# VectorE's small steps of the differential attention as steps of their own, with four slots for the small tiles

## The chip, the cores and the metric

The kernel runs on one core of one Trainium2 chip. The metric is the device time of one execution in microseconds. The engines of the core are TensorE (PE in the rows, its weight loads PEld), VectorE (DVE), ScalarE (ACT), GpSimd (POOL) and SyncE (SP), which issues most of the transfers. Each has an instruction stream of its own; they meet only through semaphores.

## The reference, cut to what matters

The block holds projections, differential attention with 4 heads, latent attention with 4 heads, an output projection and an MLP. The change touches the differential attention alone. For one head, with 2064 keys (16 meta tokens and 2048 tokens):

```python
s1 = einsum(q1, k1) * scale + bias      # bias: ALiBi slope * distance, and the chunk mask
s2 = einsum(q2, k2) * scale + bias
a = softmax(s1) - lam * softmax(s2)
o = einsum(a, v)
```

`lam` is one number for all heads, made of two dot products and two exponentials.

## The kernel before

The queries of a head are 16 tiles of 128 rows, i = 0 to 15, in four groups g of four tiles. Tile i sees 16 + 128*(i+1) keys (144 for tile 0, 2064 for tile 15). Each tile has two components c (`s1` and `s2`), and each component's scores are cut into chunks of at most 512 columns: one chunk for tiles 0 to 2, two for 3 to 6, three for 7 to 10, four for 11 to 14, five for 15. That makes 88 chunks a head, numbered 0 to 87: tile 3 begins at chunk 6, tile 7 at 22, tile 8 at 28, tile 11 at 46, tile 12 at 54, tile 13 at 62, tile 14 at 70, tile 15 at 78.

What the engines do for one tile:

- TensorE makes a chunk's scores in one of four PSUM banks (line 1609, two passes of fp32r). Before chunk n it waits until VectorE has read chunk n - 4.
- VectorE reads a chunk out of its bank (line 1531): it adds the bias, writes the row into SBUF and keeps the chunk's maximum. After a component's last chunk it makes the negative maximum of the row (line 1538).
- ScalarE takes the exponential of the row in place and sums it (line 1477). This needs the maximum.
- "scale": VectorE makes the inverse of the first sum (`invert`, line 1563); GpSimd multiplies the first row by it (line 1469).
- "end": VectorE makes the inverse of the second sum (line 1570), multiplies it by minus lambda (line 1572), and adds the second row, times that, to the first (line 1576, one pass over the whole row).
- "turn": TensorE transposes the finished rows of a group, one key tile at a time (line 1642), into one of three banks; ScalarE copies it out (line 1490). The first turn of group g waits for the end of its last tile, 4g + 3.
- "product": TensorE multiplies the transposed tile with the values (line 1656), and ScalarE copies the group's sum out ("out", line 1497).

Group 3 of a head has its turns and products beside the first rows of the next head. All engines follow one list of steps, made by `row_steps` (the order of chunks, exponentials, scales and ends) and `head_steps` (which spreads turns and products over it by a cost of each step). Each engine walks the list and does its own kinds of step. A step of a row is put off by a number of chunks: the exponential 1, the scale `SCALE_AFTER` = 2, the end `END_AFTER` = 5; at the last chunk of a component of tile i, whatever is still due for tiles below i is put there at once. The first turn of a group is held back in the list until the end that it needs has passed.

Rows of the first component lie in `rows`; those of the second in `second`, which has two slots, tile i in slot i % 2. The small tiles `mx`, `nmax`, `total`, `inv` and `inv2` have two slots as well.

Of the kernel before, what the change touches and what calls it, by code (L numbers as in the profile page):

```python
# [30 lines left out]
P = 128  # L31
D = 1024
SEQ = 2048
META = 16
# [1128 lines left out]
def attention(nc, io, scr, ident, ahead, latent):  # L1163
# [8 lines left out]
    with ExitStack() as ctx:  # L1172
# [10 lines left out]
        mx = mem.sb("da_mx", [P, 2, COMPS, 5])  # L1183
        nmax = mem.sb("da_nmax", [P, 2, COMPS])
        nmax_all = mem.sb("da_nmax_all", [P, 5])
        total = mem.sb("da_total", [P, 2, COMPS])
        inv = mem.sb("da_inv", [P, 2, COMPS])
        inv2 = mem.sb("da_inv2", [P, 2])
# [15 lines left out]
        inv2_step = mem.sem("da_inv2_step")  # L1204
# [58 lines left out]
        def cost(step):  # L1263
# [3 lines left out]
            return META + P * (step[2] + 1) + 250 if step[0] == "end" else 0  # L1267
# [47 lines left out]
        SCALE_AFTER, END_AFTER = 2, 5  # L1315
# [146 lines left out]
        def _(pool):  # L1462
# [3 lines left out]
            def scaled(h, i, u, **at):  # L1466

                hold(pool, inv_ready, NT * h + i + 1)
                pool.tensor_scalar(row(i, u), row(i, u), inv[:, i % 2, 0:1], 1.0, ALU.mult, ALU.mult).then_inc(first_scaled, 1)
# [4 lines left out]
        def _(act):  # L1474
            def exp(h, i, c, u, **at):
                act.wait_ge(max_ready, NT * COMPS * h + COMPS * i + c + 1)
                act.activation(comp_row(i, c, u), comp_row(i, c, u), ACT.Exp, bias=nmax[:, i % 2, c:c + 1], scale=scale,
                               accum_out=total[:, i % 2, c:c + 1]).then_inc(exp_ready, 1)
# [32 lines left out]
        def _(dve):  # L1511
            def chunk(h, n, pair, u):
# [7 lines left out]
                if i % 4 == 0 and c == 0 and k0 == 0:  # L1520
# [4 lines left out]
                    elif g != 1 and not first_head:  # L1525
# [3 lines left out]

                hold(dve, scores_ready, NCH * h + n + 1)  # L1530
# [3 lines left out]
                                         accum_out=mx[:, i % 2, c, nth:nth + 1]).then_inc(scores_read, 1)  # L1534
                if k0 + w == META + P * (i + 1):
                    dve.wait_ge(scores_read, NCH * h + n + 1)

# [1936 lines left out]
```

## Time and profile before

| | us |
|---|---|
| median of 3 runs | 2602.93 |
| lowest, highest | 2600.15, 2602.96 |
| profiled execution, from its first to its last instruction | 2600.7 |
| differential attention in it | 432 to 799 |
| latent attention, output projection, MLP | from 802 on |

The page gives the profiled execution's own time as its span, and nothing that lies around it. In the whole span TensorE is busy for 98%, VectorE 62%, ScalarE 47%, GpSimd 13%. Times of rows are microseconds from the span's start. In the timeline rows the columns are start, duration, engine, line, operation, result and operands with the shape, how many were merged into the row, and in brackets the idle time before it with the engine that ended it. TensorE's passes are pipelined: a transposition seen alone takes 0.27 us, four in a row 0.60 us.

### The profile page before, as it was taken

How to read it: one execution, taken by the hardware profiler on the slowest of the kernel's cores; microseconds unless marked ns; L12 is line 12 of the kernel's file. 1: busy time of each engine (PE TensorE's matmuls, PEld its weight loads, DVE VectorE, ACT ScalarE, POOL GpSimd, SP SyncE). 2: the span in 40 equal slices, each digit the busy share in tenths (PEclk: the TensorE clock that was granted, in tenths of full speed). 3: DMA queues.
4: the chain of work that ended last, by engine and by line, in shares of the span. 5: the costliest groups of instructions: out<-in, count | busy, mean ns of one | idle time of the engine just before them, and what ended most of it. 6: DMA issues, size and time to landing. Idle time of an engine off the chain costs nothing.

```text
span 2600.7 us, 35372 instructions
## 1 busy us (share of the span) xinstructions
PE 2540.5 (98%) x12220; PEld 2114.9 (81%) x12220; DVE 1614.7 (62%) x3499; ACT 1212.5 (47%) x2183; POOL 332.0 (13%) x368
## 2 busy tenths in 40 slices
PE   8999999999999999999999999999999999999997
PEld 7998888777667999977877888888888888888886
DVE  6123306998995776654458677876757465564765
ACT  6112314777764555554544333533335353443554
POOL 1110002222221222210000000000000001111143
PEclk9999999999999999999999999999999999999999
DMA  7334458553332111135677767657655365776787
GB/s 232 122 106 125 126 163 253 143 135 87 93 131 90 36 31 45 41 110 158 194 247 220 221 200 237 218 182 216 190 161 179 110 221 108 171 167 162 203 162 137
DMA packets 329436, 398.59 MB, mean 153 GB/s; under 512 B 21408, under 2 KB 235664, under 8 KB 320944
## 3 DMA queue, kind: packets, MB, share of 16 engines
q1 hardware_dynamic: 311696, 364.41, 44.7%
q0 software_dynamic: 17568, 31.99, 8.4%
q8 instruction: 95, 1.56, 0.2%
q14 instruction: 77, 0.63, 0.1%
HBM read 239.86 MB, written 156.48 MB: 152 GB/s over the span
## 4 chain that ended last, share of the span: by engine, by line
PE 62%; DVE 3%; DMA 1%; ACT 1%; issue 1%; SPq 0%; POOL 0%; DVEq 0%; ACTq 0%; POOLq 0%
PE ff_ps_x L3262 26%; PE ff_ps_m L3262 13%; PE ff_ps_z L3262 6%; PE ml_ps_s L2139 6%; PE ff_ps_m L1695 4%; PE ml_ps_o L2168 4%; PE ml_ps_t L2152 2%; DMA ml_v_raw<-scr_yT 1%; DMA ff_pieces<-scr_acc 0%; PE ff_ps_r L2699 0%; PE mo_ps_t L2716 0%; SPq L2326 0%; DVE ff_pieces L2429 0%; DVE ff_pieces L2620 0%; DVE ff_pieces L2616 0%
## 5 line engine op out<-in xcount | busy, mean ns | idle before, releaser
L3262 PE MATMUL ff_ps_x<-ff_mv_hi_p,ff_st_hi_p 128*128 128x512 f32 x764 | 297.8, 390 | 0.5 <-ACT ff_u L3002 0.5
L3262 PE MATMUL ff_ps_x<-ff_mv_hi_p,ff_st_lo_p 128*128 128x512 f32 x764 | 297.3, 389 | 0.0
L3262 PE MATMUL ff_ps_x<-ff_mv_lo_p,ff_st_hi_p 128*128 128x512 f32 x764 | 297.2, 389 | 0.0
L2139 PE MATMUL ml_ps_s<-wide,ml_qs 128*128 128x416 f32 (+14 forms) x880 | 195.6, 356 | 3.7 <-PEq L137 2.7
L3108 DVE TENSOR_TENSOR ff_st_lo_p<-ff_ps_m,ff_st_hi_p 128x512 fp32r<-128x512 f32 x190 | 130.8, 689 | 103.4 <-ACT ff_st_hi_p L2985 103.4
L2952 POOL DMA_DIRECT2D scr_acc<-ff_pieces x64 | 55.5, 872 | 1015.3 <-DVE ff_pieces L3132 946.9
L3002 ACT ACTIVATE ff_u<-ff_ps_x 128x512 f32<-128x512 f32 x128 | 76.6, 598 | 215.0 <-PE ff_ps_x L3262 215.0
L3262 PEld LDWEIGHTS ff_ps_x<-ff_mv_hi_p,ff_st_hi_p 128*128 128x128 f32 x764 | 143.4, 188 | 32.4 <-issue 2.0
L3262 PEld LDWEIGHTS ff_ps_x<-ff_mv_hi_p,ff_st_lo_p 128*128 128x128 f32 x764 | 143.4, 188 | 29.9
L3262 PEld LDWEIGHTS ff_ps_x<-ff_mv_lo_p,ff_st_hi_p 128*128 128x128 f32 x764 | 143.4, 188 | 29.6
L2139 PEld LDWEIGHTS ml_ps_s<-wide,ml_qs 128*128 128x128 f32 x880 | 152.0, 191 | 16.3 <-issue 2.9
L2985 ACT ACTIVATE ff_st_hi_p<-st_raw 128x512 fp32r<-128x512 f32 x191 | 119.4, 626 | 86.3 <-PE ff_ps_z L3262 86.3
L3262 PE MATMUL ff_ps_m<-wide,ff_st_hi_p 128*128 128x512 f32 x512 | 157.7, 389 | 0.4 <-DVE ff_st_lo_p L2603 0.4
L2985 ACT ACTIVATE ff_st_hi_p<-ff_ps_m 128x512 fp32r<-128x512 f32 x190 | 113.2, 598 | 93.7 <-PE ff_ps_m L3262 93.7
L3262 PE MATMUL ff_ps_x<-wide,ff_st_hi_p 128*128 128x512 f32 x504 | 155.1, 389 | 0.0
L3108 DVE TENSOR_TENSOR ff_st_lo_p<-st_raw,ff_st_hi_p 128x512 fp32r<-128x512 f32 x191 | 131.0, 688 | 36.9 <-ACT ff_st_hi_p L2985 35.6
L2054 DVE CUSTOM_DVE_ANT_0 ml_rows<-ml_ps_s,ahead_bias 128x416 f32<-128x416 f32 (+14 forms) x176 | 100.2, 570 | 72.1 <-PE ml_ps_s L2139 64.2
L1656 PE MATMUL da_ps_o<-da_pT,da_v 128*128 128x512 f32 (+3 forms) x320 | 137.2, 529 | 0.0
L1977 ACT ACTIVATE ml_pT_hi<-ml_ps_t 128x512 fp32r<-128x512 f32 (+3 forms) x176 | 90.7, 538 | 93.4 <-PE ml_ps_t L2152 93.0
L2076 DVE TENSOR_TENSOR ml_pT_lo<-ml_ps_t,ml_pT_hi 128x512 fp32r<-128x512 f32 (+3 forms) x176 | 105.3, 616 | 41.6 <-ACT ml_pT_hi L1977 41.2
L1609 PE MATMUL da_ps_s<-da_keys,ahead_q 128*128 128x416 f32 (+14 forms) x352 | 112.6, 423 | 2.4 <-DVE da_mx L1531 2.4
L3262 PEld LDWEIGHTS ff_ps_m<-wide,ff_st_hi_p 128*128 128x128 f32 x512 | 96.0, 188 | 20.5 <-issue 0.6
(318 smaller groups left out, 6349.7 us busy)
## 6 DMA issues: line engine op xcount, KB each, us to landing
st_raw<-in_w_ff SPq DMA_DIRECT2D x64, 512.0 KB, 6.2
scr_hid<-ff_pieces SPq DMA_DIRECT2D x128, 256.0 KB, 2.7
st_raw<-scr_hid SPq DMA_DIRECT2D x64, 512.0 KB, 5.4
ring<-in_w_ff SPq DMA_DIRECT2D x28, 1024.0 KB, 7.7
scr_t<-ring SPq DMA_DIRECT2D x24, 1024.0 KB, 5.8
ring<-scr_t SPq DMA_DIRECT2D x21, 1024.0 KB, 8.1
scr_acc<-ff_pieces POOLq DMA_DIRECT2D x64, 256.0 KB, 4.1
ring<-scr_u SPq DMA_DIRECT2D x13, 1024.0 KB, 8.4
```

What stands on the lines that cost most here:

```text
L1609: m = pe.matmul(ps_s[n % NSB][:, 0:w], qs[:, g % 2, c, P * b:P * b + P], keys[u][:, 2 * c + j, k0:k0 + w], start=j == 0, stop=j == 1)
L1656: pe.matmul(ps_o[:, c0:512], v_meta[:, :] if t == 0 else v[:, t - 1], pT[0:rows_of, n % NPT, c0:512], start=t == 0, stop=t == tiles_of(g) ...
L1695: m = pe.matmul(bank, y[a][:, k], w[b][:, cols], start=k == 0 and i == 0, stop=k == KD - 1 and i == 2, skip_group_check=True)
L1977: act.activation(pT_hi[0:rows_of, n % NPT, c0:512], ps_t[n % NTB][0:rows_of, c0:512], ACT.Copy).then_inc(hi_copied, 1)
L2054: dve.tensor_tensor_reduce(out=row(i, u)[:, k0:k0 + w], in0=ps_s[n % NSB][:, 0:w], in1=bias[:, b0:b0 + w], scale=1.0, scalar=LOWEST, op0=A ...
L2076: dve.tensor_tensor(pT_lo[0:rows_of, n % NPT, c0:512], ps_t[n % NTB][0:rows_of, c0:512], f32(pT_hi[0:rows_of, n % NPT, c0:512]), ALU.subtr ...
L2139: m = pe.matmul(ps_s[n % NSB][:, 0:w], q, k, start=j == 0, stop=j == len(pairs) - 1)
L2168: m = pe.matmul(ps_o[:, c0:512], v[0:rows_of, at_v], p, start=t == 0 and j == 0, stop=t == tiles_of(g) - 1 and j == 2)
L2985: act.activation(st_hi[kind][:, :, :], stationary(kind, n % 2), ACT.Copy).then_inc(st_hi_ready, 1)
L3002: act.activation(tile, bank[:, :], ACT.Copy).then_inc(taken, 1)
L3108: dve.tensor_tensor(st_lo[kind][:, :, :], stationary(kind, n % 2), f32(st_hi[kind][:, :, :]), ALU.subtract).then_inc(st_lo_ready, 1)
L3262: m = pe.matmul(bank[:, :], w[kind][:, k], a[kind][:, k], start=start and k == 0 and i == 0, stop=stop and k == KH - 1 and i == 2, skip_gr ...
```

## The change

It has three parts.

1. The negative maximum of a row becomes a step of its own, "most". It was made right behind the last chunk of a component; now one chunk later, right ahead of its exponential. Its long output goes back into `mx`, and `nmax_all` is dropped.
2. The end is cut in three: "invert" (the second inverse), "weigh" (the product with minus lambda) and "end" (the addition), each put off by one chunk more than the one before. The invert is put off by 5 chunks for tile 15, 3 for tiles 0 to 2, else by two less than the number of chunks of the next tile's two components, at most 6; so the addition comes 2 chunks after that. `SCALE_AFTER` becomes 3. What is still due at a component's last chunk is put there only from one tile further back than before in the first component, and not at all for tiles 0 to 2.
3. The small tiles get four slots (i % 4), and the rows of the second component of tiles 0 to 2 lie side by side in slot 0. Since in-order work no longer guards the second rows, VectorE waits for `probs_ready` ahead of the first chunk of each second component.

In the planner the cost of an end falls from its width + 250 to its width + 100.

```diff
-        mx = mem.sb("da_mx", [P, 2, COMPS, 5])
+        mx = mem.sb("da_mx", [P, 4, COMPS, 5])
...
         def comp_row(i, c, u):
-            return row(i, u) if c == 0 else second[:, i % 2, 0:META + P * (i + 1)]
+            if c == 0:
+                return row(i, u)
+            start, wide = (sum(META + P * (a + 1) for a in range(i)), 0) if i < 3 else (0, i % 2)
+            return second[:, wide, start:start + META + P * (i + 1)]
...
-                        steps += [step for _, step in later if step[2] - NT * step[1] < i]
-                        later = [(left, step) for left, step in later if step[2] - NT * step[1] >= i]
-                        later.append((1, ("exp", 0, i, c)))
+                        due = i if c == COMPS - 1 else i - 1
+                        if i < 3:
+                            due = -1
+                        steps += [step for _, step in later if step[2] - NT * step[1] < due]
+                        later = [(left, step) for left, step in later if step[2] - NT * step[1] >= due]
+                        later += [(1, ("most", 0, i, c)), (1, ("exp", 0, i, c))]
                         if c == 0:
                             later.append((SCALE_AFTER, ("scale", 0, i)))
                         if c == COMPS - 1:
-                            later.append((END_AFTER, ("end", 0, i)))
+                            later += [(after, (kind, 0, i)) for kind, after in zip(("invert", "weigh", "end"), end_after(i))]
...
+        def end_after(i):
+            first = {NT - 1: 5, 0: 3, 1: 3, 2: 3}.get(i) or min(6, 2 * len(row_chunks(i + 1)) - 2)
+            return first, first + 1, first + 2
...
-        SCALE_AFTER, END_AFTER = 2, 5
+        SCALE_AFTER = 3
...
+                if c == 1 and k0 == 0 and not (first_head and i < 4):
+                    dve.wait_ge(probs_ready, NT * h + (-1 if i < 3 else 0 if i == 3 else i - 1))
...
+            def most(h, i, c, **at):
+                last = max(n for n, chunk in enumerate(chunks) if chunk[:2] == (i, c))
+                parts = len(row_chunks(i))
+                dve.wait_ge(scores_read, NCH * h + last + 1)
+                dve.tensor_scalar(mx[:, i % 4, c, 0:parts], mx[:, i % 4, c, 0:parts], -scale, None, ALU.mult, ALU.min,
+                                  accum_out=nmax[:, i % 4, c:c + 1]).then_inc(max_ready, 1)
...
+            def invert_second(h, i, **at):
+                dve.wait_ge(exp_ready, NT * COMPS * h + COMPS * (i + 1))
+                dve.reciprocal(inv[:, i % 4, 1:2], total[:, i % 4, 1:2]).then_inc(second_inverted, 1)
+
+            def weigh_second(h, i, **at):
+                dve.wait_ge(second_inverted, NT * h + i + 1)
+                dve.tensor_scalar(inv2[:, i % 4:i % 4 + 1], inv[:, i % 4, 1:2], lam[:, 3:4], None, ALU.mult).then_inc(second_weighed, 1)
+
+            def end(h, i, u, **at):
+                dve.wait_ge(second_weighed, NT * h + i + 1)
+                dve.wait_ge(first_scaled, NT * h + i + 1)
+                dve.scalar_tensor_tensor(out=row(i, u), in0=comp_row(i, 1, u), scalar=inv2[:, i % 4:i % 4 + 1], in1=row(i, u),
+                                         op0=ALU.mult, op1=ALU.add).then_inc(probs_ready, 1)
```

## Rows read from the trace of the kernel before

**Rows 1.** The page's first part: busy time and share of the span.

```profile
PE 2540.5 (98%) x12220; PEld 2114.9 (81%) x12220; DVE 1614.7 (62%) x3499; ACT 1212.5 (47%) x2183; POOL 332.0 (13%) x368
```

**Rows 2.** Window within the differential attention: stretch, busy time by engine, clock, DMA.

```profile
602.00:685.00 83.00, 80.06 (x407) 59.48 (x406) 76.78 (x293) 60.73 (x108) 17.72 (x16) 1.00 0.45 108
```

**Rows 3.** Waits from 432 to 775: who, for whom, us, times, longest.

```profile
ACT da_second L1477 <- DVE da_nmax_all L1538: 44.0, 39, 2.9
DVE da_inv L1570 <- ACT da_second L1477: 6.7, 4, 2.2
PE da_ps_s L1609 <- DVE da_mx L1531: 6.1, 10, 1.1
```

**Rows 4.** Timeline of PE: what its passes take, and two waits further in.

```profile
458.36 1.92 PE L1609 MATMUL da_ps_s<-wide,ahead_q 128*128 128x336 f32 x10
460.12 0.60 PE L1642 MATMUL da_ps_t<-ident,da_rows 128*128 128x128 f32 x4
...
463.63 0.67 PE L1609 MATMUL da_ps_s<-wide,ahead_q 128*128 128x448 f32 x2 [1.07 <-DVE da_mx L1531]
...
561.22 0.64 PE L1609 MATMUL da_ps_s<-da_keys,ahead_q 128*128 128x416 f32 x2 [0.45 <-DVE da_mx L1531]
...
586.24 1.02 PE L1656 MATMUL da_ps_o<-da_pT,da_v 128*128 128x512 f32 x2
```

**Rows 5.** Timeline of PE where head 1 ends and head 2 starts.

```profile
597.15 0.63 PE L1609 MATMUL da_ps_s<-da_keys,ahead_q 128*128 128x400 f32 x2 [0.75 <-DVE da_mx L1531]
...
604.43 1.09 PE L1642 MATMUL da_ps_t<-ident,da_rows 128*128 128x128 f32 x8 [1.26 <-DVE da_rows L1576]
...
607.07 1.12 PE L1656 MATMUL da_ps_o<-da_pT,da_v_meta 128*128 128x512 f32 x2 [0.48 <-ACT da_pT L1490]
```

**Rows 6.** Timeline of DVE over the same change of heads.

```profile
597.52 0.09 DVE L1531 DVE_READ_ACCUMULATOR2_ANT da_mx<- 128x1 f32 x1
597.52 0.16 DVE L1563 RECIPROCAL da_inv<-da_total 128x1 f32<-128x1 f32 x1
597.60 0.57 DVE L1531 CUSTOM_DVE_ANT_0 da_second<-da_ps_s,da_bias 128x416 f32<-128x416 f32 x1
...
598.09 0.59 DVE L1531 CUSTOM_DVE_ANT_0 da_second<-da_ps_s,da_bias 128x416 f32<-128x416 f32 x1
...
599.10 0.09 DVE L1531 DVE_READ_ACCUMULATOR2_ANT da_mx<- 128x1 f32 x1
599.22 0.16 DVE L1538 TENSOR_SCALAR_CACHE_REDUCE da_nmax_all<-da_mx 128x5 f32<-128x5 f32 x1
599.30 0.08 DVE L1538 DVE_READ_ACCUMULATOR da_nmax_all<-da_mx 128x1 f32 x1
...
601.56 0.16 DVE L1570 RECIPROCAL da_inv<-da_total 128x1 f32<-128x1 f32 x1 [1.61 <-ACT da_second L1477]
601.76 0.21 DVE L1572 TENSOR_SCALAR da_inv<-da_inv,da_lam 128x1 f32<-128x1 f32 x1
602.01 2.37 DVE L1576 SCALAR_TENSOR_TENSOR da_rows<-da_second,da_inv,da_rows 128x2064 f32<-128x2064 f32 x1
604.29 0.30 DVE L1531 CUSTOM_DVE_ANT_0 da_second<-da_ps_s,ahead_bias 128x144 f32<-128x144 f32 x1
```

**Rows 7.** Timeline of DVE: chunk 57 of head 1, which had to wait for its scores.

```profile
571.13 0.51 DVE L1531 CUSTOM_DVE_ANT_0 da_rows<-da_ps_s,da_bias 128x336 f32<-128x336 f32 x1 [0.42 <-PE da_ps_s L1609]
```

**Rows 8.** Timeline of ACT over the same change of heads.

```profile
599.42 2.02 ACT L1477 ACTIVATE da_second<-da_second,da_nmax 128x2064 f32<-128x2064 f32 x1 [2.65 <-DVE da_nmax_all L1538]
601.34 0.19 ACT L1477 ACTIVATION_READ_ACCUMULATOR da_second<-da_second,da_nmax 128x1 f32 x1
601.44 0.40 ACT L1477 ACTIVATE da_rows<-da_rows,da_nmax 128x144 f32<-128x144 f32 x1
```

**Rows 9.** Windows at the end of the stage, where PE stands idle and starts again.

```profile
775.00:778.00 3.00, 0.68 (x6) 0.68 (x7) 2.97 (x3) 0.18 (x1) 0.00 (x0) 1.00 0.25 94
778.00:782.00 4.00, 4.00 (x15) 2.72 (x14) 3.60 (x7) 1.86 (x4) 0.00 (x0) 0.57 0.32 68
```

More of the change, by code:

```diff
@@ L1182, in attention @@
         pT = mem.sb(f"da_pT", [P, NPT, 512])
-        mx = mem.sb("da_mx", [P, 2, COMPS, 5])
[L1184 to L1188, printed above, removed]
+        mx = mem.sb("da_mx", [P, 4, COMPS, 5])
+        nmax = mem.sb("da_nmax", [P, 4, COMPS])
+        total = mem.sb("da_total", [P, 4, COMPS])
+        inv = mem.sb("da_inv", [P, 4, COMPS])
+        inv2 = mem.sb("da_inv2", [P, 4])
         lam = mem.sb("da_lam", [P, 4])
@@ L1203, in attention @@
         inv_ready, first_scaled, probs_ready = (mem.sem(f"da_{s}") for s in ("inv_ready", "first_scaled", "probs_ready"))
-        inv2_step = mem.sem("da_inv2_step")
+        second_inverted, second_weighed = mem.sem("da_second_inverted"), mem.sem("da_second_weighed")
         pT_ready, pv_done = mem.sem(f"da_pT_ready"), mem.sem("da_pv_done")
@@ L1266, in cost @@
                 return chunks[step[2]][3] + 60
-            return META + P * (step[2] + 1) + 250 if step[0] == "end" else 0
+            return META + P * (step[2] + 1) + 100 if step[0] == "end" else 0
         def head_steps():
@@ L1468, in scaled @@
                 hold(pool, inv_ready, NT * h + i + 1)
-                pool.tensor_scalar(row(i, u), row(i, u), inv[:, i % 2, 0:1], 1.0, ALU.mult, ALU.mult).then_inc(first_scaled, 1)
+                pool.tensor_scalar(row(i, u), row(i, u), inv[:, i % 4, 0:1], 1.0, ALU.mult, ALU.mult).then_inc(first_scaled, 1)
             heads(pool, {"scale": scaled})
@@ L1476, in exp @@
                 act.wait_ge(max_ready, NT * COMPS * h + COMPS * i + c + 1)
-                act.activation(comp_row(i, c, u), comp_row(i, c, u), ACT.Exp, bias=nmax[:, i % 2, c:c + 1], scale=scale,
-                               accum_out=total[:, i % 2, c:c + 1]).then_inc(exp_ready, 1)
+                act.activation(comp_row(i, c, u), comp_row(i, c, u), ACT.Exp, bias=nmax[:, i % 4, c:c + 1], scale=scale,
+                               accum_out=total[:, i % 4, c:c + 1]).then_inc(exp_ready, 1)
                 if isinstance(h, int) and (h, i, c) == (0, 0, 1):
@@ L1555, in minus_lambda, with invert_first @@
                 dve.wait_ge(lam_step, 4)
-            def invert(h, i, u, **at):
+            def invert_first(h, i, u, **at):
                 dve.wait_ge(exp_ready, NT * COMPS * h + COMPS * i + 1)
-                if not (isinstance(h, int) and h == 0 and i < 2):
-                    dve.wait_ge(first_scaled, NT * h + i - 1)
-                dve.reciprocal(inv[:, i % 2, 0:1], total[:, i % 2, 0:1]).then_inc(inv_ready, 1)
-            def end(h, i, u, **at):
+                if not (isinstance(h, int) and h == 0 and i < 4):
+                    dve.wait_ge(first_scaled, NT * h + i - 3)
+                dve.reciprocal(inv[:, i % 4, 0:1], total[:, i % 4, 0:1]).then_inc(inv_ready, 1)
@@ L1574, in end @@
                 dve.wait_ge(first_scaled, NT * h + i + 1)
-                dve.scalar_tensor_tensor(out=row(i, u), in0=comp_row(i, 1, u), scalar=inv2[:, i % 2:i % 2 + 1], in1=row(i, u),
+                dve.scalar_tensor_tensor(out=row(i, u), in0=comp_row(i, 1, u), scalar=inv2[:, i % 4:i % 4 + 1], in1=row(i, u),
                                          op0=ALU.mult, op1=ALU.add).then_inc(probs_ready, 1)
-            heads(dve, {"chunk": chunk, "scale": invert, "end": end})
+            heads(dve, {"chunk": chunk, "most": most, "scale": invert_first, "invert": invert_second, "weigh": weigh_second, "end": end})
```

12 lines of the change are left out of this document (1 added, 11 removed).

## The prediction

> **What bounds the kernel now.** I read the page's busy shares first, then windows over the stage of the change, then the waits, then the timelines of the engines where one head meets the next. Over the whole span TensorE is the busy one [rows 1]. In the stage of the change it is busy for 80.06 of 83 us and VectorE for 76.78 [rows 2]: two engines, both near their limit, so each needs its own sum. The waits go both ways: TensorE for VectorE's reads 6.1 us, VectorE for ScalarE's exponential 6.7, ScalarE for VectorE's maxima 44.0 [rows 3].
>
> TensorE's work of a head. Ten score passes take 1.92 us, of which the last 0.30 is a tail, so a pass costs 0.18 us; four transpositions take 0.60 us and one alone 0.27, so one costs 0.11; a product is two passes, 0.43 apart (1.02 less the 0.59 of one), so 0.86 at full width [rows 4]. A head has 176 score passes (31.7 us), 152 transpositions (16.7 us), and products worth 38 full ones (32.7 us): 81 us. The four heads take 343 us from 432 to 775, 85.8 each. TensorE thus stands still for some 4.7 us a head.
>
> Where it does, in a head further in: ahead of chunk 87 (0.75 us, waiting for VectorE), ahead of the first turn of group 3 (1.26, waiting for the end of tile 15), ahead of that group's first product (0.48, for ScalarE's copy) [rows 5], and ahead of chunk 47 (0.45) [rows 4]. Each costs some 0.25 more than it prints, because after a gap the overlap of passes is lost: 1.0, 1.5, 0.75 and 0.7. With small ones of 0.6 in all (chunks 0, 70 and 79) that makes 4.6. Head 0 has no old group to turn, and loses 1.3 ahead of chunk 35 (1.07 printed) [rows 4], 0.7 ahead of chunk 47, and 1.0 in its first ten chunks. After the last head it waits 3.0 for the last end. Sum up to 777 us: 3.0 in head 0, 0.4 in each of the four third groups, 3.5 at each of three changes of head, 2.2 at chunk 47 of three heads, 4.0 at the close: 21.3 us. Nothing that the change does to VectorE can give back more.
>
> VectorE's work of a head. A read costs its columns at 0.96 per ns plus 0.08, about 0.5 us for 416 (chunk at 597.60, next at 598.09). A maximum costs 0.24: the read's accumulator goes out at 599.10, the maximum starts at 599.22, its own accumulator at 599.30, the next work 0.04 later. An end costs 0.45 before its long pass (601.56 to 602.01), then its columns plus 0.1 [rows 6]. A head: 43.8 for reads, 32 maxima 7.7, 16 inverses 1.2, 16 ends 27.2, together 80 us.
>
> **What the change does to VectorE.** The 0.12 between 599.10 and 599.22 is the wait for its own result: an inverse that has nothing to wait for starts in the same instant as the accumulator before it, and costs 0.08 (597.52 to 597.60) [rows 6]. One chunk later, the maximum has nothing to wait for either: 0.085 in place of 0.24, 5.0 us over 32. The inverse and the lambda product of an end fall from 0.45 to 0.08 plus the product's cost by itself, which no row shows; it lies between 0.08 (as an inverse) and 0.25 (its start to the addition's, with the wait), and I take 0.13, nearer to an operation without a wait: 3.9 us over 16. VectorE's head goes from 80 to 71 us, 36 us less over the stage (31 to 37 by the two ends). The added wait ahead of each second component costs nothing: the end that it asks for lies three or more chunks back in the list. The copy of the maximum into `mx` and the four slots move no work. ScalarE gets each maximum one read (0.5 us) later, and the copies queued behind its exponentials with it; its 44.0 us of waiting for maxima [rows 3] cover that, since a product asks for a copy two or more turns back. SyncE's loads and GpSimd's scaling wait for counts that come no sooner and, by 1 us at most, later; GpSimd is idle most of the time.
>
> The page "VectorE: DVE Perf Modes" of the Trainium skill, section "The DRAIN you can't avoid", speaks against this saving: a next operation starts only when the pipe is empty, and a semaphore in between "costs nothing extra". The row shows 0.12 us where there is a wait and nothing where there is none, so I go by the row; by the page the sum of VectorE would stay at 80 us.
>
> **What it does to TensorE.** VectorE was not alone in setting the pace, so its 36 us aren't the gain. At chunk 57 it already waits 0.42 for scores [rows 7]; with less work it sits directly behind TensorE over most of a head, and TensorE stops only where an order of steps makes it. I walked the new list with the costs above, in four places.
>
> Chunk 47 and head 0. The end of tile 9 comes after chunk 45 in place of 42, and VectorE is 3 us ahead of where it was. The 0.7 at chunk 47 goes in all heads, and about 1.1 of the 2.3 that head 0 loses in its first ten chunks and at chunk 35: 3.9 us gained.
>
> Chunk 61. The end of tile 11 is put off from chunk 57 to chunk 61, and the first turn of group 2, which was at 60, is held back to stand right behind it. VectorE starts to read chunk 61 0.15 us after its scores at best and some 0.6 with the lag that I get; the read costs 0.43, the addition 1.72. TensorE has 0.65 us of products left and then stands until that end: 2.7 less 0.65, 2.1 us (1.6 at best). It did not wait here before. Four heads: 8.4 us lost. ScalarE has the copies of group 1 behind it and adds nothing.
>
> Chunks 70 to 85. The scale of tiles 11 to 14 is two chunks behind the maximum, 1.2 to 1.4 us of work, and asks for an exponential of up to 2.0 us: VectorE now stands here for some 0.6 us at tiles 13 and 14, where an end used to cover it. TensorE, up to four banks ahead, loses 0.3 a head, as much as it did before (0.4). Even.
>
> The change of heads. With the end of TensorE's chunk 85 as zero: VectorE has read it at 1.8, makes the end of tile 14 (2.1), which was at chunk 82 before, and reads 86, 87 and chunk 0 of the next head until 5.2. The maximum of tile 15 follows at 5.3; before it was at 4.2, ahead of chunk 0. The exponential with its accumulator, from there to the inverse, takes 2.3 (599.22 to 601.56), and that of tile 0 another 0.4 [rows 6, 8]. VectorE's scale of tile 0, which the list has ahead of all that is left of tile 15, waits for it until 7.9: the 1.61 of idle time returns in another place. Then it has chunks 4, 5 and 6 and nine small steps, 2.2 us, and only then the end of tile 15, 2.25 with its tail: 12.5. TensorE has by then chunks 86 to 6 of the next head and eight products, three of them narrow, 8.2 us. It stands still for 4.3 us, in two pieces (0.7 ahead of chunk 2, which needs the bank of chunk 86, the rest ahead of the first turn). Three turns then stand before the first product, so the 0.75 for the copy goes. 4.3 against 3.5: three times 0.8 lost, 2.4 us. At the close of the last head VectorE reads chunk 87 1.1 later and TensorE has 1.0 more work to hide it: even.
>
> Sum: -3.9 + 8.4 + 0 + 2.4 - 0.4 (the small ones) = +6.5 us. What follows, from 777 on, only moves: no transfer of those stages ends a wait of TensorE's in this one. The page gives the profiled execution as 2600.7 us and nothing around it; the median is 2602.9, so I set 2609.
>
> **Rivals.** Faster: VectorE's reads decide after all. If VectorE's 9 us a head let it stand right behind TensorE at chunk 61 and at the change of heads too, its lateness costs nothing: the waits ahead of chunks 35, 47 and 87 go (1.3 + 2.8 + 4.0), the small ones too (1.6), and the two new ones shrink to what the end itself takes; 2594. For it: both waits for `da_mx` ahead of chunks 47 and 87 are of this kind. Against: an end of 2 us still stands in one piece before the first turns. It decides if the new wait at chunk 61 is under 0.5 us. Chance 0.25.
>
> No change: the lag behind TensorE is 0.15 in place of what I carried (-0.4 a head at chunk 61, -1 at the change of heads), some 5 us less: 2603. Chance 0.29.
>
> Slower still, by the clock: TensorE's idle time of 2.8 us at 775 is followed by a stretch at 0.57 of its clock, half speed in most of 4 us [rows 9], a loss of some 1.7 us; the 1.5 us of idle time at 604 is not. I get 3.6 in one piece at three changes of head: +5, 2614. Chance 0.12, as the piece may be shorter.
>
> That waits cost VectorE nothing, as the page has it: the ends are later by the same chunks, and the path from chunk 57 to the end of tile 15 grows by what I had taken off it, ten maxima by 0.155 and five ends by 0.25, 2.8 us: +11, 2620. The 0.12 of the row would then be something else. Chance 0.04.
>
> **Numbers.** My forecast (chance 0.30): 2609, in a range of its own of 2605 to 2612. A measurement of this kernel tells some 0.2%, 5.2 us, from no change: faster is below 2597.7, slower above 2608.1. The two cases above the forecast lie in slower, with three quarters of the forecast's; the rest of it, the no-change case and a fifth of the faster one lie within: faster 0.21, same 0.41, slower 0.38. The range runs from 2593, the faster rival, to 2616, past the clock's.
>
> **What would show it.** Right: reads right after `TENSOR_SCALAR_CACHE_REDUCE` with no 0.12 before it, VectorE's busy time in the stage some 20 us lower; a wait of PE for `da_rows` in every head between the product of width 128 after chunk 61 and the first turn, some 2 us; one of over 2.5 at the change of heads; no wait ahead of chunk 47. Wrong: no wait at chunk 61, or waits for `da_mx` that add up to more than now.

## The result, and the profile after

The changed kernel takes 2637.78 us (median of four runs, 2635.87 to 2639.6), the kernel before 2601.54 in the same comparison: a ratio of 1.0142 [1.013, 1.0154]. It is 36 us slower. The forecast of 2609 had the direction and a fifth of the size, and the time lies 22 us outside its range.

All of it is lost in the stage of the change. From the first scores of the differential attention to the first of the latent attention the trace of before takes 369.9 us (432.2 to 802.1), that of after 405.1 (431.8 to 836.9). The 1798 us behind it are alike. The windows of the stage in the trace of before (length; busy us and instructions of PE, PEld, DVE, ACT, POOL; granted clock; DMA share; GB/s):

```profile
432.00:802.00 370.00, 353.14 (x1738) 260.47 (x1736) 318.94 (x1232) 260.72 (x463) 77.42 (x67) 1.00 0.47 124
```

The page's busy line of the kernel after, which answers to [rows 1], hides it: the shares are within a point of the old ones.

```profile
PE 2551.9 (97%) x12220; PEld 2124.8 (81%) x12220; DVE 1621.2 (62%) x3499; ACT 1213.2 (46%) x2183; POOL 335.6 (13%) x368
```

The windows of the same trace show it, first the stretch that answers to [rows 2], then the whole stage:

```profile
602.00:685.00 83.00, 73.54 (x359) 54.37 (x358) 69.38 (x270) 54.41 (x101) 17.45 (x15) 0.97 0.47 115
...
432.00:837.00 405.00, 360.87 (x1736) 267.18 (x1736) 325.68 (x1231) 260.22 (x462) 78.00 (x67) 0.97 0.42 113
```

TensorE is busy for 73.5 of 83 us where it was busy for 80.1 [rows 2]. VectorE's busy time in the stage was to fall by some 20 us. It rose, from 318.94 to 325.68. That one number says that something has become slower, for the change takes no pass away from GpSimd and adds none to VectorE.

The waits from 432 to 810 (engine and line waiting, releaser: us, times, longest) have the one of TensorE for the finished rows, which was not among those of any size in [rows 3]. ScalarE's for the maxima is up from 44.0 us:

```profile
ACT da_second L1487 <- DVE da_mx L1556: 59.5, 36, 3.6
...
PE da_ps_t L1661 <- DVE da_rows L1595: 22.1, 7, 3.9
PE da_ps_s L1628 <- DVE da_mx L1544: 14.3, 12, 1.8
```

VectorE's timeline from the inverse of tile 11 on (start, us, engine, line, operation, result and operands; idle time and its releaser in brackets) shows both halves of the story:

```profile
575.00 0.16 DVE L1579 RECIPROCAL da_inv<-da_total 128x1 f32<-128x1 f32 x1 [0.43 <-ACT da_rows L1487]
575.12 0.47 DVE L1544 CUSTOM_DVE_ANT_0 da_second<-da_ps_s,da_bias 128x304 f32<-128x304 f32 x1
575.52 0.08 DVE L1544 DVE_READ_ACCUMULATOR2_ANT da_mx<- 128x1 f32 x1
575.52 2.87 DVE L1595 SCALAR_TENSOR_TENSOR da_rows<-da_second,da_inv,da_rows 128x1424 f32<-128x1424 f32 x1
578.32 0.61 DVE L1544 CUSTOM_DVE_ANT_0 da_rows<-da_ps_s,da_bias 128x448 f32<-128x448 f32 x1
578.86 0.07 DVE L1544 DVE_READ_ACCUMULATOR2_ANT da_mx<- 128x1 f32 x1
578.86 0.14 DVE L1556 TENSOR_SCALAR_CACHE_REDUCE da_mx<-da_mx 128x4 f32<-128x4 f32 x1
...
583.03 0.21 DVE L1589 TENSOR_SCALAR da_inv<-da_inv,da_lam 128x1 f32<-128x1 f32 x1
583.15 0.15 DVE L1579 RECIPROCAL da_inv<-da_total 128x1 f32<-128x1 f32 x1
```

The small steps do what they were said to: the maximum starts in the same instant as the accumulator before it (578.86), with no 0.12 between them, and the lambda product costs 0.12 (583.03 to 583.15; 0.13 was assumed). But the addition over 1424 columns (tile 10) takes 2.87 us, where the same form took 1.70 before. The prediction's rule, columns at 0.96 per ns and 0.1, gives 1.58 up to the start of the next operation, which comes some 0.1 us ahead of the printed end. GpSimd in the same stretch:

```profile
575.33 1.58 POOL L1479 TENSOR_SCALAR da_rows<-da_rows,da_inv 128x1552 f32<-128x1552 f32 x1 [3.35 <-DVE da_inv L1579]
```

GpSimd's scaling of tile 11 (1552 columns) begins 0.2 us ahead of VectorE's addition for tile 10 and ends at 576.91; the addition is longer than its 1.70 by 1.17, out of 1.39 us beside each other. The additions of tiles 13 to 10, once in each of the four heads, in the groups by form (count, busy us, mean ns, idle before), ahead of the change:

```profile
L1576 DVE SCALAR_TENSOR_TENSOR da_rows<-da_second,da_inv,da_rows 128x1808 f32<-128x1808 f32 x4 | 8.4, 2101 | 0.1
L1576 DVE SCALAR_TENSOR_TENSOR da_rows<-da_second,da_inv,da_rows 128x1680 f32<-128x1680 f32 x4 | 7.9, 1970 | 0.1
L1576 DVE SCALAR_TENSOR_TENSOR da_rows<-da_second,da_inv,da_rows 128x1552 f32<-128x1552 f32 x4 | 7.3, 1835 | 0.1
L1576 DVE SCALAR_TENSOR_TENSOR da_rows<-da_second,da_inv,da_rows 128x1424 f32<-128x1424 f32 x4 | 6.8, 1703 | 0.1
```

and after it:

```profile
L1595 DVE SCALAR_TENSOR_TENSOR da_rows<-da_second,da_inv,da_rows 128x1808 f32<-128x1808 f32 x4 | 13.9, 3482 | 0.0
L1595 DVE SCALAR_TENSOR_TENSOR da_rows<-da_second,da_inv,da_rows 128x1680 f32<-128x1680 f32 x4 | 13.1, 3266 | 0.0
L1595 DVE SCALAR_TENSOR_TENSOR da_rows<-da_second,da_inv,da_rows 128x1552 f32<-128x1552 f32 x4 | 12.3, 3081 | 0.0
L1595 DVE SCALAR_TENSOR_TENSOR da_rows<-da_second,da_inv,da_rows 128x1424 f32<-128x1424 f32 x4 | 11.5, 2870 | 0.0
```

From 7.61 us a head to 12.70: 5.1 more, 20.4 over four heads. Of the others only that of tile 15 is longer by more than 0.02 us, 2.44 for 2.37. Why these four: the scale stood two chunks behind its maximum and now stands three behind, the ends moved as well, and the two have met: for i = 11 to 14 the list now has the scale of tile i right ahead of the addition of tile i - 1.

Where that comes out is TensorE's timeline. From the first turn of group 2 in head 1 to the first of group 3:

```profile
582.13 0.81 PE L1675 MATMUL da_ps_o<-da_pT,da_v 128*128 128x256 f32 x4
...
586.82 0.66 PE L1661 MATMUL da_ps_t<-ident,da_rows 128*128 128x128 f32 x4 [3.87 <-DVE da_rows L1595]
...
608.57 1.75 PE L1628 MATMUL da_ps_s<-da_keys,ahead_q 128*128 128x400 f32 x6 [1.83 <-DVE da_mx L1544]
...
615.19 0.52 PE L1628 MATMUL da_ps_s<-wide,ahead_q 128*128 128x272 f32 x2 [1.30 <-DVE da_mx L1544]
...
623.16 1.53 PE L1661 MATMUL da_ps_t<-ident,da_rows 128*128 128x128 f32 x12 [2.34 <-DVE da_rows L1595]
```

After the narrow products these are idle pieces of one head: ahead of the first turn of group 2, ahead of chunk 82, and two at the change of heads. Counted from the ends of passes, as in the prediction, a head further in loses 4.1 us ahead of the first turn of group 2, 0.8 and 2.1 in chunks 70 to 85, 0.5 at chunk 49, 1.6 ahead of chunk 2 and 2.6 ahead of the first turn of group 3: 11.7 in place of 4.6, some 28 us over four heads. The rest of the 35 is the clock. The window behind the first of these waits:

```profile
586.00:592.00 6.00, 5.18 (x23) 4.63 (x24) 3.13 (x10) 3.47 (x5) 0.00 (x0) 0.72 0.43 103
```

Inside it, from 588.1 to 591.5, the granted clock is 0.50. Such stretches, of 3.4 us if nothing else is said, begin at 492.5, 588.1, 680.2 (6.8 us long), 779.2 and 813.4, 20 us in all, each behind a wait of TensorE's (the one at 680.2 begins 1.8 us before its wait ends); the kernel before has one in the stage, of 3.4 us at 778.1 [rows 9]. Half speed over 17 us more is at most 8.5 us of work lost, and 28 + 8.5 is the 35 to within 2. The two windows of the whole stage divide it alike: TensorE's idle time rises from 16.9 to 44.1 us, its busy time from 353.1 to 360.9.

### The profile page after: what moved, and what is told of

Same layout as the page of the kernel before. It is cut to its first block, busy times and chain, and to the rows that moved or that the text cites. A ratio compares the mean times of both kernels' runs of the same rounds, so it can differ in the third digit from the quotient of the medians.

```text
span 2634.1 us, 35370 instructions
## 1 busy us (share of the span) xinstructions
PE 2551.9 (97%) x12220; PEld 2124.8 (81%) x12220; DVE 1621.2 (62%) x3499; ACT 1213.2 (46%) x2183; POOL 335.6 (13%) x368
## 3 DMA queue, kind: packets, MB, share of 16 engines
q8 instruction: 95, 1.56, 0.2%
## 4 chain that ended last, share of the span: by engine, by line
PE 61%; DVE 2%; DMA 1%; ACT 1%; issue 1%; SPq 0%; POOL 0%; DVEq 0%; ACTq 0%; POOLq 0%
PE ff_ps_x L3281 25%; PE ff_ps_m L3281 13%; PE ff_ps_z L3281 6%; PE ml_ps_s L2158 6%; PE ff_ps_m L1714 4%; PE ml_ps_o L2187 4%; PE ml_ps_t L2171 2%; DMA ml_v_raw<-scr_yT 1%; DMA ff_pieces<-scr_acc 0%; PE ff_ps_r L2718 0%; PE mo_ps_t L2735 0%; SPq L2345 0%; DVE ff_pieces L2448 0%; DVE ff_pieces L2639 0%; DVE ff_pieces L2635 0%
## 5 line engine op out<-in xcount | busy, mean ns | idle before, releaser
L1628 PE MATMUL da_ps_s<-da_keys,ahead_q 128*128 128x416 f32 (+14 forms) x352 | 120.1, 441 | 7.4 <-DVE da_mx L1544 7.4
L1661 PE MATMUL da_ps_t<-ident,da_rows 128*128 128x128 f32 x608 | 95.5, 281 | 25.6 <-DVE da_rows L1595 25.6
```

The source lines that it names most:

```text
L1628: m = pe.matmul(ps_s[n % NSB][:, 0:w], qs[:, g % 2, c, P * b:P * b + P], keys[u][:, 2 * c + j, k0:k0 + w], start=j == 0, stop=j == 1)
L1661: m = pe.transpose(ps_t[n % NTB][0:rows_of, P * b:P * b + P], row(4 * g + b, u)[:, k0:k0 + rows_of], ident[:, :])
```

## The experiments

Theory C (collision): a pass of GpSimd that has started makes the addition beside it wait. Theory O (order): the ends' new places alone cost TensorE the time. All edits are to the changed kernel; where one stands on top of another, the text says so. A difference between two experiments is one of their medians, unless the profiled executions are named.

**The scale behind the addition.** The scale of tiles 11 to 14 is put off by one chunk more, which puts it behind the addition of the tile before.

```diff
-                            later.append((SCALE_AFTER, ("scale", 0, i)))
+                            later.append((4 if 11 <= i <= 14 else SCALE_AFTER, ("scale", 0, i)))
```

> The changed kernel, with the scale of tiles 11 to 14 put off by one chunk more, so that it stands right behind the addition of the tile before instead of right ahead of it. Theory (two engines at one port): in the changed kernel GpSimd's pass over a row starts 0.2 us before VectorE's addition, and the addition of tiles 10 to 13 takes 2.87 to 3.48 us instead of 1.70 to 2.10; apart again they take 1.7 to 2.1, which gives back at least the 20.4 us that were added, and with TensorE's half-clock stretches some 25: 2610 to 2617. Rival (the order of steps alone costs the time, the long additions are hidden behind TensorE): all waits and all ends stay where they are, so 2630 or more.

Measured: 2616.85 us, ratio 1.0058 [1.0043, 1.0074]: 21 us come back. The longest of the four additions, by form:

```profile
L1595 DVE SCALAR_TENSOR_TENSOR da_rows<-da_second,da_inv,da_rows 128x1808 f32<-128x1808 f32 x4 | 8.4, 2099 | 0.0
```

And the timelines of VectorE and then of GpSimd, where tile 10's addition and tile 11's scale now follow one another:

```profile
570.14 1.70 DVE L1595 SCALAR_TENSOR_TENSOR da_rows<-da_second,da_inv,da_rows 128x1424 f32<-128x1424 f32 x1
...
572.43 0.62 DVE L1544 CUSTOM_DVE_ANT_0 da_rows<-da_ps_s,da_bias 128x448 f32<-128x448 f32 x1
```

```profile
572.07 1.56 POOL L1479 TENSOR_SCALAR da_rows<-da_rows,da_inv 128x1552 f32<-128x1552 f32 x1 [5.34 <-DVE da_inv L1579]
```

The read at 572.43 lies wholly beside GpSimd's pass and takes 0.62, as such reads do elsewhere (0.61 at 578.32 above). It has one operand in PSUM and one in SBUF; the addition has two in SBUF. Only the latter waits.

This is what the Trainium skill says on its page "SBUF — State Buffer", section "SBUF: two separate sides": VectorE with two SBUF inputs and GpSimd share a pair of ports, whichever starts first has it for its whole instruction, and "the other fully blocks". The trace of after agrees in place and, roughly, in size: the addition is 1.17 us longer for 1.39 us beside each other, 0.2 less than a block to the pass's end would give.

**GpSimd's pass made short.** The order of after is kept, and GpSimd scales only 16 columns; the rest of the scaling is left out.

```diff
-                pool.tensor_scalar(row(i, u), row(i, u), inv[:, i % 4, 0:1], 1.0, ALU.mult, ALU.mult)
+                pool.tensor_scalar(row(i, u)[:, 0:16], row(i, u)[:, 0:16], inv[:, i % 4, 0:1], 1.0, ALU.mult, ALU.mult)
```

> The changed kernel in its own order, with GpSimd's scaling done on 16 columns of each row instead of all of them (this part of the computation is left out). Theory (port): every addition takes what it takes alone, 1.70 us for 1424 columns and 2.10 for 1808, and the time falls by over 20 us, to 2608 to 2616. Rival (the additions are slow for what stands on VectorE itself, a wait or the new place of the rows): they stay at 2.9 to 3.5 us and the time within 3 us of 2638.

Measured: 2617.63, ratio 1.0062 [1.0047, 1.0078]. The additions by form:

```profile
L1595 DVE SCALAR_TENSOR_TENSOR da_rows<-da_second,da_inv,da_rows 128x1808 f32<-128x1808 f32 x4 | 8.4, 2097 | 0.0
...
L1595 DVE SCALAR_TENSOR_TENSOR da_rows<-da_second,da_inv,da_rows 128x1424 f32<-128x1424 f32 x4 | 6.8, 1697 | 0.0
```

With the order untouched the additions are back at their old length and the time is that of the experiment before. For these 20 us it is GpSimd's duration beside the additions that costs, not where the ends stand. Theory C holds for 21 of the 36 us.

**The old order with the new steps.** Splits and four slots stay; the places of scale and end are the old ones.

```diff
-                        due = i if c == COMPS - 1 else i - 1
-                        if i < 3:
-                            due = -1
+                        due = i
-            first = {NT - 1: 5, 0: 3, 1: 3, 2: 3}.get(i) or min(6, 2 * len(row_chunks(i + 1)) - 2)
+            first = 3
-            return META + P * (step[2] + 1) + 100 if step[0] == "end" else 0
+            return META + P * (step[2] + 1) + 250 if step[0] == "end" else 0
-        SCALE_AFTER = 3
+        SCALE_AFTER = 2
```

> The steps and the slots of the change, in the order of before: the maximum one chunk later, invert, weigh and end 3, 4 and 5 chunks behind, scale at 2, dues and costs as before. Theory: the splits save VectorE 9 us a head, and with the ends where they were TensorE loses none of the new waits, so the waits for VectorE's reads go: 2592 to 2597, ratio 0.996 to 0.998. Rival (a wait costs VectorE nothing): ratio 1.000, and the maximum still starts 0.1 us late. Second rival (the maximum one chunk later makes ScalarE late): slower, by up to 5 us.

Measured: 2675.24, ratio 1.029 [1.0276, 1.0304], the slowest of all. The theory and the first rival were wrong; the second rival had the direction, with 5 us at most where it became 75. The waits of the stage:

```profile
DVE da_inv L1577 <- ACT da_rows L1485: 56.9, 64, 1.7
...
DVE da_inv L1581 <- ACT da_second L1485: 44.8, 64, 2.2
```

VectorE now stands at each of the 64 first inverses and each of the 64 second ones for its exponential. The maximum comes a chunk later, so the exponential does; the scale that stayed two chunks behind the row has one chunk to wait out in place of two. `SCALE_AFTER = 3` belongs to the split; I had taken order and split to be separable. TensorE stands still for 58.6 of the stage's 443.3 us and is busy for 384.7 where it was for 353.1: with the waits came 51 us at half speed. The test of this reading is further down.

**Scale and tile 11's end.** The first experiment, with the end of tile 11 taken back to chunk 58.

```diff
-            first = {NT - 1: 5, 0: 3, 1: 3, 2: 3}.get(i) or min(6, 2 * len(row_chunks(i + 1)) - 2)
+            first = {NT - 1: 5, 0: 3, 1: 3, 2: 3, 11: 3}.get(i) or min(6, 2 * len(row_chunks(i + 1)) - 2)
```

> The first experiment of this set and, besides, the end of tile 11 put off by 5 chunks in all (chunk 58) instead of 8 (chunk 61). Theory: TensorE's wait ahead of the first turn of group 2 (4.1 us in the changed kernel, some 2.5 in the first experiment) goes in all four heads, 6 to 9 us less than the first experiment: 2602 to 2609. Rival (TensorE makes up for that wait later, because VectorE is the bound): within 2 us of the first experiment.

Measured: 2602.04 (ten runs, 2599.45 to 2606.69), ratio 1.0007 [0.9998, 1.0016]. The first turn of group 2, as the first experiment has it and as this one has it:

```profile
579.99 1.05 PE L1661 MATMUL da_ps_t<-ident,da_rows 128*128 128x128 f32 x4 [2.52 <-DVE da_rows L1595]
```

```profile
575.93 0.66 PE L1661 MATMUL da_ps_t<-ident,da_rows 128*128 128x128 f32 x4 [0.20 <-DVE da_rows L1595]
```

The wait of 2.5 us is down to 0.2. In the four heads the first experiment prints 2.17, 2.52, 2.17 and 2.17, so about 8.2 us go with them. The half-speed stretches of the stage are 17 us in the one trace and 13.6 in the other, up to 1.7 us more, and the profiled executions are 9.1 apart (2614.0 and 2604.9). The medians are 14.8 apart, and the rest goes with the clock: of the ten executions of this kernel the four with a mean granted clock of 0.994 took 2605.5 to 2606.7 us, the profiled one among them, and the six with 0.996 or 0.997 took 2599.5 to 2602.4. The four of the first experiment have 0.990, 0.992, 0.994 and 0.996 and took 2619.6, 2618.0, 2615.7 and 2609.6. Why the clock falls in one execution and not in the next is not shown.

**Tile 15's end sooner as well**, behind chunk 4 of the next head in place of 6.

```diff
-            first = {NT - 1: 5, 0: 3, 1: 3, 2: 3, 11: 3}.get(i) or min(6, 2 * len(row_chunks(i + 1)) - 2)
+            first = {NT - 1: 3, 0: 3, 1: 3, 2: 3, 11: 3}.get(i) or min(6, 2 * len(row_chunks(i + 1)) - 2)
```

> The kernel of the last experiment (scale of tiles 11 to 14 behind the sum, tile 11's end at chunk 58) with the end of tile 15 put off by 5 chunks instead of 7: behind chunk 4 of the next head, where it was behind chunk 6. Theory (TensorE waits 2.6 us at each change of heads only for where this end stands): the end comes 1.5 us sooner, three times, and TensorE's wait ahead of the first turn falls to about 1.0 us: 4 to 6 us less than before this edit, 2596 to 2599 where that kernel took 2602. Rival (VectorE has to wait for the exponential of tile 15 wherever the end stands): within 2 us of 2602.

Measured: 2598.06 (eleven runs), ratio 0.999 [0.9981, 0.9999], the lowest of all kernels, 0.1% below the one before. It is 4.0 us below the kernel that it stands on, as the theory had it, though the two intervals just touch. TensorE's timeline at its change of heads:

```profile
596.30 0.52 PE L1628 MATMUL da_ps_s<-wide,ahead_q 128*128 128x272 f32 x2 [1.20 <-DVE da_mx L1544]
...
602.91 0.66 PE L1661 MATMUL da_ps_t<-ident,da_rows 128*128 128x128 f32 x4 [1.60 <-DVE da_rows L1595]
```

Its stage by windows:

```profile
432.00:799.00 367.00, 349.17 (x1734) 261.11 (x1732) 302.44 (x1231) 258.66 (x462) 77.46 (x67) 0.99 0.47 125
```

VectorE is busy for 302.4 us in the stage, 16.5 fewer than before (318.94), and the stage is 2.6 us shorter (431.2 to 798.5).

**Tile 14's end sooner too**, behind chunk 83 in place of 85 (`14: 4` in the same table).

```diff
-            first = {NT - 1: 3, 0: 3, 1: 3, 2: 3, 11: 3}.get(i) or min(6, 2 * len(row_chunks(i + 1)) - 2)
+            first = {NT - 1: 3, 0: 3, 1: 3, 2: 3, 11: 3, 14: 4}.get(i) or min(6, 2 * len(row_chunks(i + 1)) - 2)
```

> The same and, besides, the end of tile 14 two chunks sooner, behind chunk 83 instead of 85. Theory: VectorE's 2.1 us addition then no longer stands between the reads of chunks 85 and 86, and TensorE's 1.5 us of waiting ahead of chunk 2 of the next head goes, 3 to 4 us less than with tile 15 alone: 2592 to 2596, faster than both kernels. Rival (the addition only moves, and TensorE then waits ahead of chunk 87 as in the kernel before, 1.0 us): 1 to 2 us less.

Measured: 2610.85, ratio 1.0041 [1.0027, 1.0055]: a loss of 12 us where a gain was expected. VectorE's timeline:

```profile
685.02 2.23 DVE L1595 SCALAR_TENSOR_TENSOR da_rows<-da_second,da_inv,da_rows 128x1936 f32<-128x1936 f32 x1
687.16 0.15 DVE L1556 TENSOR_SCALAR_CACHE_REDUCE da_mx<-da_mx 128x5 f32<-128x5 f32 x1
...
689.50 0.16 DVE L1579 RECIPROCAL da_inv<-da_total 128x1 f32<-128x1 f32 x1 [1.15 <-ACT da_rows L1487]
```

The end fell right ahead of the maximum of tile 15's first component, held it up by 2.2 us, and with it the exponential and the inverse that waits 1.15 us for it. TensorE's idle time in the stage is 4.5 us longer than without this edit (22.3 and 17.8), its busy time 7.0 (355.7 and 348.7): behind two waits close together, of 1.3 and 1.4 us, the granted clock is 0.50 for 3.4 us at all three changes of head (from 512.6, 601.4 and 690.1), which the kernel without this edit does not have.

**The maximum at once**, to weigh that split alone (to the kernel with scale and tile 11's end mended): `most` is called right behind the last read, as before the change.

```diff
+                if k0 + w == META + P * (i + 1):
+                    most(h, i, c)
-            heads(dve, {"chunk": chunk, "most": most, "scale": invert_first, "invert": invert_second, "weigh": weigh_second, "end": end})
+            heads(dve, {"chunk": chunk, "scale": invert_first, "invert": invert_second, "weigh": weigh_second, "end": end})
```

> The kernel of the last experiment of the first set (2602), with the maximum made right behind a component's last chunk again, in the same order of all other steps. It costs VectorE 0.155 us more each, 5 us a head, and gives ScalarE the maximum one read sooner. Theory (the split of the maximum brings nothing here, since TensorE is the bound and the exponential is what VectorE waits for): 2599 to 2603. Rival (VectorE's time counts): 2607 or more.

Measured: 2604.35, ratio 1.002 [1.0011, 1.003], 1.4 us above the range of the theory. The split of the maximum is worth 2.3 us by the medians; the intervals (that of its base reaches 1.0016) overlap, so it is not shown to be worth anything.

**The end in one piece**, on the same base: inverse and product stand right ahead of the addition again, with their waits.

```diff
+                invert_second(h, i)
+                weigh_second(h, i)
-            heads(dve, {"chunk": chunk, "most": most, "scale": invert_first, "invert": invert_second, "weigh": weigh_second, "end": end})
+            heads(dve, {"chunk": chunk, "most": most, "scale": invert_first, "end": end})
```

> The same kernel (2602), with invert and weigh right ahead of the addition again, each waiting for the one before, 0.25 us more for each of 16 ends of a head, the rest in the same order. Theory (only what stands ahead of a first turn or of a bank counts): 1 to 3 us more, 2603 to 2605. Rival (VectorE's time counts in full, 4 us a head): 2610 or more. Second rival (the sooner invert makes VectorE wait for exponentials and is itself the loss): 2600 or less.

Measured: 2609.15, ratio 1.0035 [1.0021, 1.0049]. This split is worth 7 us, more than the theory had and just under the rival's 2610. The intervals, up to 1.0016 and from 1.0021, are apart.

**Tile 14's end behind the maximum** (`14: 5`, behind chunk 84), to tell order from place in the loss above, and **tile 15's end behind chunk 3** (`NT - 1: 2`) on top of it.

```diff
-            first = {NT - 1: 3, 0: 3, 1: 3, 2: 3, 11: 3}.get(i) or min(6, 2 * len(row_chunks(i + 1)) - 2)
+            first = {NT - 1: 3, 0: 3, 1: 3, 2: 3, 11: 3, 14: 5}.get(i) or min(6, 2 * len(row_chunks(i + 1)) - 2)
```

> The kernel with tile 15's end behind chunk 4 (2598), with the end of tile 14 behind chunk 84 instead of 85. In the run that put it behind 83 it stood ahead of tile 15's maximum and made ScalarE's exponential, and with it the scale of tile 15, late (1.15 us of VectorE's idle time). Theory (that order was the loss, not the sooner end): here the maximum goes first, no wait for the exponential stands ahead of chunk 86, and TensorE's 1.5 us ahead of chunk 2 falls to about 1.0: 2594 to 2598. Rival (any sooner end of tile 14 costs): 2601 or more.

> The same with the end of tile 15 behind chunk 3. Theory: it stands ahead of the scale of tile 0 and its addition starts 0.6 us sooner; TensorE's wait ahead of the first turn falls from 1.8 to about 1.2 us: 1 to 3 us less than with chunk 4. Rival (its inverse at chunk 1 makes VectorE wait for the exponential before it has read chunks 2 and 3, and TensorE runs out of banks): 1 to 4 us more.

Measured: 2600.08, ratio 0.9997 [0.9988, 1.0006], and 2598.74, ratio 0.9995 [0.9986, 1.0004]. One chunk later, behind the maximum, the 11 us are back: it was the order, which set off the longer waits and the half-speed stretches behind them. The first lies between its theory (up to 2598) and its rival (from 2601) and decides nothing on the sooner end; the second is 1.3 us below it, as its theory had it. Neither can be told from the best kernel, nor from the kernel before: no place of the ends that was tried from here on gains anything that can be measured.

**The old order, with the maximum at once.** The third experiment with the edit of the seventh, `most` right behind the last read: if the late maximum made it slow, this cures it.

> The run that had the new steps in the order of before (2675), with the maximum made right behind the last chunk again; invert and weigh stay steps of their own. Theory (its loss was the maximum one chunk later with the scale still at 2: 64 waits for the first exponential of 0.9 us each and 64 for the second of 0.7): the waits for the first exponential fall to a few, those for the second by half, 2598 to 2608. Rival (the loss came from inverses that stand ahead of the reads): 2640 or more.

Measured: 2604.69, ratio 1.0012 [1.0003, 1.0022]; 70.6 us come back by one edit, as the theory had it. The waits:

```profile
DVE da_inv L1583 <- ACT da_second L1485: 10.4, 12, 2.2
...
DVE da_inv L1579 <- ACT da_rows L1485: 2.5, 3, 0.8
```

The 56.9 and 44.8 us are 2.5 and 10.4.

**The collision put back into the best kernel**, to size it where nothing else waits.

```diff
-                            later.append((4 if 11 <= i <= 14 else SCALE_AFTER, ("scale", 0, i)))
+                            later.append((SCALE_AFTER, ("scale", 0, i)))
```

> The kernel with tile 15's end behind chunk 4 (2598), with the scale of tiles 11 to 14 put back by one chunk, right ahead of the addition, as in the change. Theory (port): GpSimd's pass then meets three additions a head (tiles 10, 12 and 13; tile 11's stands elsewhere), 1.2 to 1.4 us each, 15.4 us in all, and most of it is on the path: 2608 to 2616, with tile 11's addition at 1.83 us. Rival (in an order without the two long waits TensorE covers it): within 3 us of 2598.

Measured: 2619.05, ratio 1.007 [1.0056, 1.0084], 21 us slower than without and 3 above the range of the theory. Its additions by form:

```profile
L1595 DVE SCALAR_TENSOR_TENSOR da_rows<-da_second,da_inv,da_rows 128x1808 f32<-128x1808 f32 x4 | 13.9, 3481 | 0.0
L1595 DVE SCALAR_TENSOR_TENSOR da_rows<-da_second,da_inv,da_rows 128x1680 f32<-128x1680 f32 x4 | 13.1, 3263 | 0.0
L1595 DVE SCALAR_TENSOR_TENSOR da_rows<-da_second,da_inv,da_rows 128x1424 f32<-128x1424 f32 x4 | 11.4, 2862 | 0.0
...
L1595 DVE SCALAR_TENSOR_TENSOR da_rows<-da_second,da_inv,da_rows 128x1552 f32<-128x1552 f32 x4 | 7.3, 1831 | 0.0
```

Tile 11's end (1552 columns) has moved off tile 12's scale and is short; the other three (tiles 10, 12 and 13) collide and carry 15.4 us. The time lost is more than that. The stage by windows:

```profile
432.00:818.00 386.00, 354.74 (x1732) 261.39 (x1730) 318.25 (x1231) 258.36 (x462) 77.10 (x66) 0.99 0.45 118
```

VectorE is busy for 318.2 us in place of 302.4, 15.8 more, nearly all of it the 15.4. TensorE stands still for 31.3 (386.0 less 354.7) and for the 1.6 us behind this window too, up to the latent attention's first scores at 819.6: 32.9 in place of 17.8, so 15 us reach it as waits. One more stretch at half speed (from 692.4 to 695.8) is up to 1.7 of the rest. The remaining 4 or so lie in TensorE's busy time, where passes that follow a wait have lost their overlap; that is a reading of the sums, and no run here shows it alone.

## Why the prediction was right or wrong

**VectorE's savings, 0.155 a maximum and some 0.25 an end: right.** No 0.12 before the maxima, 0.12 for the product. Its busy time in the best kernel is 16.5 us lower; the prediction's 36 us also counted gaps between instructions. The Trainium skill's page "VectorE: DVE Perf Modes", section "The DRAIN you can't avoid", says of eight copies in a row that a semaphore behind each "costs nothing extra". For these small steps the traces do not agree: the 0.12 us are there with the wait (599.10 to 599.22, before) and gone without it (578.86, after). It was right as well to price the gain at less than VectorE's saving: the split of the end is worth 7 us and that of the maximum 2.3 by medians that can't be told apart, not 36.

**"An end costs its columns plus 0.1": this failed.** It is the step that carries the miss: beside GpSimd the additions of tiles 10 to 13 cost 1.17 to 1.38 us more than they did, 20.4 us in all. The prediction moved the scale against the ends in the list and looked only at what the inverse waits for; "GpSimd is idle most of the time" took the engine's load for harmlessness. What counts is whether GpSimd's pass has begun when the addition starts. The terms for chunk 61 and the chunks 70 to 85 carried 2.1 and 0.3 a head; with the collision they measured 4.1 and 2.9. The first and the last experiment give the missing term as 21 us, twice. One of the prediction's own signs of being wrong came true with it: TensorE's waits for `da_mx` add up to 14.3 us, where they were 6.1 [rows 3], and VectorE's busy time rose where it was to fall by 20.

**Chunk 61, 2.1 a head: right.** With no collision the turn waits 2.2 to 2.5 us in each head, and taking the end back removes it (2602.04). The forecast had this term, 8.4 us; without it the time falls by 14.8, since the clock goes with the waits.

**The change of heads, 4.3 for 3.5: right.** 4.1 in the kernel after, in two pieces ahead of chunk 2 and of the first turn as forecast. Moving tile 15's end two chunks forward took 4.0 us off the median.

**Chunk 47 and head 0: nearly right.** The wait ahead of chunk 47 is gone. A product at chunk 49 waits 0.48 in its place, which the prediction didn't have.

**The clock rival, chance 0.12: the mechanism came true, its condition did not.** The forecast tied it to one piece of 3.6 us at the change of heads. The piece there was 2.3 us, with no half speed behind it; it came behind chunk 61's wait instead, and 17 us more at half speed are up to 8.5 us. In the kernel without the collision the stage is 14.3 us longer than before (431.6 to 815.8). Half speed over 13.6 us more is up to 6.8 of it, which leaves 7.5 for the waits, where 6.5 was forecast. That is near, and in part by luck: the idle time alone rose by 11.3 us (16.9 to 28.2) and the busy time by 2.6, less than those 6.8, so some 4 us of busy time must have gone elsewhere, which the forecast doesn't have. The clock should have stood in the sum once it held four new waits of over 2 us.

**The faster rival, 2594**, needed the wait at chunk 61 under 0.5 us. With that wait at 0.2 the kernel takes 2602, with the change of heads mended 2598. In the best order tried VectorE's saving is worth 2 to 3.5 us (2598.06 against 2600.05 beside it and 2601.54 in the result); TensorE has 81 us of work in each 86.

In sum: 36 us are 21 for the collision, 15 for the end of tile 11 with the clock that hangs on it, and 4 for the end of tile 15, which is 40, less the 3.5 by which the kernel with all three mended is ahead of the kernel before. The 21 come out of three experiments; the 15 and the 4 out of one each.

## What to carry to other kernels

Before a step moves in a list, look at what the other engine of VectorE and GpSimd will be doing at its new place: here a pass with two SBUF operands that started 0.2 us behind a GpSimd pass paid 1.17 of the 1.39 us that were left of it, though GpSimd was busy for only 13% of the span. Taking 16.5 us of work off VectorE paid only where it ended a wait; the same change put off one end by four chunks, which made TensorE wait 2.5 us where it had waited for nothing. And a delay given to a producer (the maximum) must be given to its consumers as well: without it the same kernel ran 71 us slower. And a wait of TensorE's can cost more than its length, by the half-speed stretch behind it; that is how 4.5 us of waits became 12 us when tile 14's end moved.

## What the runs showed of the hardware

The collision goes both ways. In the kernel after, GpSimd's pass over 400 columns starts while an addition runs (VectorE, then GpSimd), and is 0.78 us long:

```profile
530.41 0.50 DVE L1595 SCALAR_TENSOR_TENSOR da_rows<-da_second,da_inv,da_rows 128x272 f32<-128x272 f32 x1
```

```profile
530.61 0.78 POOL L1479 TENSOR_SCALAR da_rows<-da_rows,da_inv 128x400 f32<-128x400 f32 x1 [5.01 <-DVE da_inv L1579]
```

The form's mean before was 0.601 us and is 0.770 after. Whichever started first kept its own duration: the 1552 columns on GpSimd took 1.58 us beside the addition and 1.56 without it. And waits of TensorE were followed by stretches at a granted clock of 0.50, of 3.4 us or twice that. In the differential attention of all traces but that of the third experiment (where waits follow one another too closely to be told apart) there are 15 waits of 3.4 us or more, and each has such a stretch, which begins within the wait or up to 1.3 us behind it. Of the 28 waits of 2.1 to 2.8 us 18 have one; in the trace of after the three of 2.3 us have none. Shorter waits have one where two of 1.3 and 1.4 us start 2.3 us apart (tile 14's end at chunk 83), and once behind a single one of 1.8 us (in the last experiment). Where TensorE is busy throughout the 3.4 us, such a wait costs up to 1.7 us more than its length. What decides between waits of the same length, no run here shows.
